# A two-layer attention and expert-lookup block: attention chunk by chunk, its second chunk inside the gather loop, and weighted sums as two products on the whole array

## The reference, cut to what matters

```python
for l in range(DEPTH):                       # 2
    proj = h @ w_in[l]                       # 1024 -> 1536: q, k, v of two branches
    oa = global_attention(rope(rms(qa)), rope(rms(ka)), va)    # 8 heads of 64, 2 kv heads
    ob = window_sink_attention(qb, kb, vb, sink[l], slopes)    # window 128, ALiBi, sink
    mix = concat(rms_norm(oa), rms_norm(ob)) @ w_o[l]
    h = layer_norm(ALPHA * h + mix)
    h = layer_norm(ALPHA * h + peer_ffn(h))

def peer_ffn(x):                             # per token
    q = x @ wq                               # 1024 -> 2048, 8 heads, two halves
    s1, s2 = top_k(q1 @ keys1, 16), top_k(q2 @ keys2, 16)
    top_s, idx = top_k(s1[:, None] + s2[None, :], 16)          # 128 experts of 16384
    a = gelu(u[idx] @ x) * softmax(top_s)
    return a @ v[idx]
```

## Time and profile before

| | us |
|---|---|
| median of 3 runs | 2925.54 (2920.96 to 2927.78) |
| the profiled execution | 2928.04 |
| its span in the profile | 2926.2 |
| first dots of layer 0 to last | 265.38 to 940.25 |
| first dots of layer 1 to last | 1160.47 to 1830.38 |

### The profile page before, as it was taken

The page is one execution under the profiler, slowest core; times in us unless marked ns, Lnnn a source line. Parts: engine busy times, 40 slices in busy tenths (PEclk is TensorE's granted clock), DMA queues, the critical chain, the costliest instruction groups (busy, mean ns, idle before and its releaser), DMA issues.

```text
span 2926.2 us, 33545 instructions
## 1 busy us (share of the span) xinstructions
PE 2148.5 (73%) x11740; PEld 1089.7 (37%) x11740; DVE 1582.8 (54%) x3254; ACT 813.4 (28%) x2292; POOL 843.2 (29%) x723
## 2 busy tenths in 40 slices
PE   6988677666766989676767666789878677667573
PEld 3657111121211559232323221568764532222221
DVE  4426857678544645888979865455552522121111
ACT  1402343433433212343343533322210111111110
POOL 1001444445432100454445553012110111222221
PEclk9889687677866989688888997899989788888887
DMA  7744999999999414999999999412112599999994
GB/s 282 263 169 159 421 422 422 420 412 395 422 422 378 194 37 160 381 421 375 413 378 403 422 421 417 159 42 74 58 62 101 210 404 401 388 391 381 382 379 146
DMA packets 130146, 891.48 MB, mean 305 GB/s; under 512 B 23216, under 2 KB 23600, under 8 KB 31792
## 3 DMA queue, kind: packets, MB, share of 16 engines
q0 software_dynamic: 86976, 553.74, 46.9%
q1 hardware_dynamic: 42992, 335.50, 28.6%
HBM read 880.21 MB, written 40.37 MB: 315 GB/s over the span
## 4 chain that ended last, share of the span: by engine, by line
PE 33%; DMA 33%; DVE 25%; ACT 4%; issue 4%; POOL 2%; SPq 1%; DVEq 0%; ACTq 0%; POOLq 0%
PE ps L155 31%; DMA ring<-in_peer_uv,idx_u 18%; DVE ring L1343 8%; DMA ring<-in_w_gu 6%; DVE arena L76 6%; DMA ring<-in_w_down 3%; ACT arena L125 3%; DMA arena<-in_w_gu 2%; PE ps L158 2%; DVE iu L113 2%; DVE arena L109 2%; DVE arena L1343 1%; DMA arena<-in_w_down 1%; DVE arena L97 1%; DMA arena<-in_peer_uv,idx_u 1%
## 5 line engine op out<-in xcount | busy, mean ns | idle before, releaser
L155 PE MATMUL ps<-ring,arena 64*64 64x512 f32 (+4 forms) x5248 | 1057.6, 764 | 475.2 <-ACT arena L125 348.0
L1343 DVE CUSTOM_DVE_ANT_0 ring<-ring,h 128x1024 f32<-128x1024 f32 x448 | 561.3, 1253 | 298.2 <-DMA ring<-in_peer_uv,idx_u 264.5
L2424 POOL DMA_INDIRECT ring<-in_peer_uv,idx_u x448 | 500.6, 1117 | 676.6 <-PE ps L155 517.4
L155 PEld LDWEIGHTS ps<-ring,arena 64*64 64x64 f32 (+3 forms) x5248 | 264.2, 158 | 1118.3 <-ACT arena L125 762.2
L155 PE MATMUL ps<-arena 128*128 128x128 f32 (+7 forms) x2760 | 471.4, 434 | 133.7 <-ACT arena L125 65.8
L125 ACT ACTIVATE arena<-arena 128x1 f32<-128x1 f32 (+3 forms) x1093 | 294.2, 269 | 812.8 <-DVE arena L1343 693.2
L155 PEld LDWEIGHTS ps<-arena 128*128 128x128 f32 (+4 forms) x2760 | 290.2, 191 | 325.4 <-ACT arena L125 150.7
L76 DVE TENSOR_TENSOR arena<-arena,ps 128x512 f32<-128x512 f32 (+1 forms) x158 | 93.6, 593 | 429.3 <-ACT arena L125 356.3
L155 PE MATMUL ps<-ring,hT 128*128 128x512 f32 (+2 forms) x896 | 310.2, 507 | 15.2 <-DVE hT L97 9.7
L125 ACT ACTIVATE arena<-ps 128x512 f32<-128x512 f32 (+5 forms) x192 | 106.4, 554 | 754.9 <-PE ps L155 707.5
L155 PEld LDWEIGHTS ps<-ring,hT 128*128 128x128 f32 x896 | 173.8, 200 | 140.9 <-issue 115.2
(11 more groups left out here) (116 smaller groups left out, 1394.6 us busy)
## 6 DMA issues: line engine op xcount, KB each, us to landing
ring<-in_w_gu SPq DMA_DIRECT2D x98, 1024.0 KB, 28.5
ring<-in_w_down SPq DMA_DIRECT2D x52, 1024.0 KB, 30.7
ring<-in_w_in SPq DMA_DIRECT2D x16, 2048.0 KB, 12.5
arena<-in_w_gu SPq DMA_DIRECT2D x30, 1024.0 KB, 29.9
ring<-in_w_mod SPq DMA_DIRECT2D x12, 2048.0 KB, 7.8
ring<-in_peer_wq SPq DMA_DIRECT2D x8, 2048.0 KB, 7.8
ring<-in_w_o SPq DMA_DIRECT2D x6, 2048.0 KB, 10.4
ring<-in_w_gates SPq DMA_DIRECT2D x12, 1024.0 KB, 4.9
```

The costliest lines, as they stand in the source:

```text
L155: return self.e.matmul(o, lhsT, rhs, start=start, stop=stop, skip_group_check=True)
L1343: v.done(v.e.tensor_tensor_reduce(out=row, in0=row, in1=h[:, n // 128, :], scale=1.0, scalar=0.0, op0=ALU.mult, op1=ALU.add, accum_out=aa[ ...
L2424: g.e.indirect_dma_start(out=landing(n), out_offset=None, in_=d["peer_uv"], in_offset=bass.IndirectOffsetOnAxis(ap=idx_u[:, n:n + 1], axis ...
```

## The change

1. `attention(l)` and the head of `peer(l)` are replaced by `first_chunk(l)`: chunk 0 alone from scores to queries and key scores, and of chunk 1 only what the other needs, the projections, keys and turned queries.
2. `second_chunk(l)`, the rest of chunk 1 (scores, powers, values, norm, output rows, layer norm, queries, key scores), becomes the first part of the background of the gather loop, one step at two n of three while n < 72.
3. `next_rows(1)`, the turned rows, projections, keys and turned queries of chunk 0 of layer 1, is the last part of the background of layer 0's loop.
4. Heads are paired in columns, so that scores of two kv heads use the two row halves of the array; the values product has the values as weights and gives the mix already turned; its mean squares come from a product with ones (`spread`).
5. The weighted sum of a gather is two products with a 128x128 diagonal, each 512 columns on the whole array.
6. Buffers move: the first block of `w_in`, the peer keys and the context's blocks go to a place in the arena (`block_p`), `w_mod` comes in halves of 1 MB into two places, and `wq` is loaded twice in each layer, once for each chunk.

```diff
 def beside(l, n):
+    if n < 72:
+        return 1 if n >= 2 and n % 3 else 0
     if l:
-        return 1 if n in range(10, 250, 3) else 0
-    return 1 if n in range(10, 246, 6) else 0
+        return 1 if n < 250 and n % 2 == 0 else 0
+    return 1 if n in range(72, LAST_ROWS, 3) or n in range(LAST_ROWS, 252, 2) else 0
...
                     for x in range(2):
-                        for r in range(2):
-                            i, o = slice(64 * r, 64 * r + 64), slice(64 * (r ^ x), 64 * (r ^ x) + 64)
-                            t = pe.mm(two[x][o, :], diagonals[n % 2][i, :], landing(n)[i, D + 512 * x:D + 512 * x + 512],
-                                      k == 0, k == 127)
+                        t = pe.mm(two[x][:, :], diagonals[n % 2], landing(l, n)[:, D + 512 * x:D + 512 * x + 512],
+                                  k == 0, k == 127)
                     pe.done(t, ("used", "gather", l, n))
...
+            def second_chunk(l):
+
+                yield
+                for br in (1, 0):
+                    scores(l, br, 1, OTHERS)
+                    yield from idle(3)
+                    turned_powers(l, br, 1, OTHERS)
+                    yield from idle(2)
+                    values(l, br, 1, OTHERS)
+                    yield
+                    spread(l, br, 1, OTHERS)
+                    yield from idle(2)
+                yield from out_rows(l, 1, OTHERS)
+                yield from idle(5)
+                turned_rows(2 * l + 1, 1, OTHERS)
+                yield
+                for hf in range(2):
+                    for i in (2 * hf, 2 * hf + 1):
+                        yield from queries(l, i, 1, OTHERS)
+                        yield
+                    key_scores(l, 1, hf, OTHERS)
+                    yield
...
             for l in range(LAYERS):
-                attention(l)
+                first_chunk(l)
                 if l:
-                    peer(l, context_states())
+                    peer(l, chain(second_chunk(l), context_states()))
                 else:
-                    peer(l, chain(context_rows(), conv_features(ctx_side, hcT, ctx_side.conv_blocks, 0, OTHERS)))
+                    peer(l, chain(second_chunk(l), context_rows(),
+                                  conv_features(ctx_side, hcT, ctx_side.conv_blocks, 0, OTHERS), next_rows(1)))
...
+                for i in range(4):
+                    block(Y_AT[l][i % 2], 4, d["peer_wq"][l, i], ("loaded", "wq", l, i, 1),
+                          after=[("used", "wq", l, i - 2, 1) if i > 1 else ("used", "w_o", l, i)])
```

More of the change, by code:

```diff
@@ L561, in attention @@
+                turned_queries(l, 1, 1, free)
+                modulation_columns(0)
+                turned_rows(2 * l + 1, 0, free)
+                for i in range(2):
+                    run(queries(l, i, 0, free))
+                key_scores(l, 0, 0, free)
                 modulation(4)
-                modulation_columns(0)
-                turned_powers(0, 0, upper)
+                run(queries(l, 2, 0, free))
                 modulation(5)
-                values(1, 0)
+                run(queries(l, 3, 0, free))
@@ new lines, in next_rows @@
+            def next_rows(l):
+                turned_rows(2 * l, 0, OTHERS)
+                yield
+                for i in range(3):
+                    yield from project(l, i, 0, OTHERS)
+                    yield
+                turned_keys(l, 1, 0, OTHERS)
+                turned_queries(l, 1, 0, OTHERS)
+                yield from idle(3)
+                turned_keys(l, 0, 0, OTHERS)
+                turned_queries(l, 0, 0, OTHERS)
+                yield
+            def peer(l, background):
@@ new lines, in next_rows @@
+            def next_rows(l):
+                take_kt(hT, ("hT", 2 * l), 0, 4)
+                a.wait_ge(*at("features stored"))
+                yield
+                yield from idle(3)
+                take_rows(l, 1, 0)
+                yield
+                yield
+                take_rows(l, 2, 0)
+                yield
+                take_keys(l, 1, 0)
+                take_queries(l, 1, 0)
+                yield from idle(3)
+                take_keys(l, 0, 0)
+                take_queries(l, 0, 0)
+                yield
@@ L2618, in rows_of, with modulate, into_p, norm_rows @@
                 return x.rearrange("(c p) n -> p c n", p=P)
-            def modulate():
-                for i in range(12):
-                    load(mod_place(i)[:, :], d["w_mod"][i], ring_sems[4 + 4 * (i % 2)], ("loaded", "w_mod", i),
-                         after=[("used", "w_mod", i - 2) if i > 1 else ("used", "w_in", 0, 1 + i)])
-            def ctx_block(i, name, before):
-                block(16, 4, d["w_in2"][i], ("loaded", "ctx", name), after=[before])
+            def modulate(*blocks):
+                for i in blocks:
+                    for half in range(2):
+                        load(mod_place(i, half)[:, :], d["w_mod"][i, :, 2048 * half:2048 * half + 2048], mod_sems[half],
+                             ("loaded", "w_mod", i, half), after=[("used", "w_mod", i - 1, half)] if i else ())
+            def into_p(src, name, after):
+                load(block_p[:, 0:src.shape[-1]], src, s_keys, name, after=after)
+            def norm_rows(r, name, l, after):
+                for x, tile in enumerate((norm_g, norm_b)):
+                    load(tile, d["rows"][r + x:r + x + 1, :].to_broadcast([P, D]), s_rows[x], ("loaded", name, l, x), after=after)
             counts = {}
@@ new lines, in sync_program @@
+                for i in range(2):
+                    block(Y_AT[l][i], 4, d["w_o"][l, i], ("loaded", "w_o", l, i), after=last)
+                into_p(d["peer_keys"][l], ("loaded", "keys", l), [("used", "w_in", l, 0)])
+                norm_rows(2 + 4 * l, "ln1", l, [("used", "ln2", 0) if l else ("used", "ln0", 0)])
+                if l == 0:
+                    modulate(1)
+                for i in range(2):
+                    block(X_AT[l][i], 4, d["peer_wq"][l, i], ("loaded", "wq", l, i, 0), after=[("used", "w_in", l, 1 + i)])
@@ new lines, in sync_program @@
+                if l:
+                    load(ctx_features, d["ctx_tab"], s_feat, ("loaded", "ctx", "features"), after=[("used", "keys", 1), ("features stored",)])
+                else:
+                    load(ctx_rows, rows_of(d["ctx"]), s_ctx, ("loaded", "ctx"), after=[("used", "wq", 0, 3, 1)])
+                    for i, (name, before) in enumerate((("Rk", ("used", "keys", 0)), ("Rv", ("used", "ctx", "Rk")),
+                                                        ("Gk", ("used", "ctx", "Rv")), ("Gv", ("used", "ctx", "Gk")))):
+                        into_p(d["w_in2"][i], ("loaded", "ctx", name), [before])
+                    into_p(d["w_in"][1, 0], ("loaded", "w_in", 1, 0), [("used", "ctx", "Gv")])
```

1080 lines of the change are left out of this document (588 added, 492 removed).

## The result

| | us |
|---|---|
| kernel before, median of the same job | 2924.74 (2920.96 to 2927.78) |
| changed kernel, median of 4 runs | 3691.43 (3687.78 to 3694.04) |
| ratio | 1.2621, 95% interval 1.2599 to 1.2643 |

The forecast was 2892, in a range of 2840 to 2952. The kernel is 26% slower, and none of the cases that the prediction priced comes near it.

What follows compares the result with a forecast made beforehand. The prediction took the gather loops as bound by DMA with 5% slack, the chain between them by PE, DVE and ACT in turn. 2928.0 - 10 - 65 + 41 = 2894 profiled, median 2892, range 2840 to 2952.

Steps and rivals of the forecast that it cites:

- the cases that the prediction priced: Forecast 2892 (chance 0.50); rivals: overlap costing almost nothing 2831 (0.15), background steps holding up gathers 2945 (0.20), lower PE clock 3063 (0.10).
- Layer 0, start: Before layer 0's gathers: first sum at 220 us, between 190 (loads hidden) and 250 (loads queue), against 276.35.
- between the layers: From layer 0's last dots to layer 1's first dots: 155.4 us in place of 220.2, a gain of 65.
- scores to mix 46, between 34 and 60: One chunk's attention before the gathers: PE work of 34 us plus waits for exponentials, scaling and the norm's power, taken as 46.
- its list there: Second chunk's work inside each gather loop: PE products and turns of 69 us, DVE some 33 us in layer 1.
- modulation blocks that wait for `in_w_mod`: Sign at layer 0's start: PE waits for modulation weights before the first sum; six half-block load waits, 29 us.
- The sum of a gather: In both gather loops: two whole-array products cost 1.81 us a gather (bounds 1.09 and 3.30), all beside transfers of 2.49.
- PE in the loops, clock 0.93: Both gather loops: PE needs some 626 us each at the upper clock; first-72-gather work was divided by a granted clock of 0.93.
- the lower clock: Rival for both loops: the granted clock stays at 0.73 to 0.85, making the kernel slower, 3063 us; chance 0.10.
- Changes of array mode: On PE in the loops: switching between 64x64 tiles and the whole array costs nothing, so dropping switches earns 0.
- Layer loops, 710 and 711: Gather loops: layer 0 takes 710 us from first sum, last dots 10 earlier; layer 1 takes 711 against 670, +41.
- lumps use up the gain: Rival for the loops: background steps stand before dots, diagonals or sums; a loop takes 737, total 2945; chance 0.20.

Runs made afterwards that it cites:

- the root kernel: The changed kernel with the POOL power in the mix norm replaced by a square root on ACT and a reciprocal on DVE, whole computation kept: 3078.47 us.
- the narrow kernels: Kernels summing each gather with four 64x64 products, such as the kernel before (2924.74 us) and the root kernel with that sum put back (3017.69 us).
- the kernel of 2987 us: The root kernel with four 64x64 products per sum, earlier load of the context's features and context steps further apart: 2987.04 us, ratio 1.0207.
- the best, at 2972.66: The kernel of 2987 us with the second chunk's 17 attention steps at every second gather and its other 30 at each gather from 38: ratio 1.0157.

## Why the prediction was wrong, by its own steps

- **Layer 0, start, and between the layers: the term that failed.** The prediction gave "scores to mix 46, between 34 and 60" with 12 us for the exponentials, "the scaling and the norm's power". The power alone is 81.9 us a branch. Eight are 656 us, 613 of the 799 us of the error, net of the cheaper root. It counted as a short wait what is an instruction on POOL that no row of PE or DVE shows; the rows that price it were POOL's. The four of the second chunk, inside the loops, it counted at nothing: its list there has PE and DVE alone. Stage by stage the changed kernel's last dots of layer 0 come at 1337 against 930, the stretch between takes 304 against 155, the loop of layer 1 950 against 711: +407, +149, +239, and +4 in the second block lead from 2894 to 3694.
- **The same two terms without the power were right.** In the root kernel the first sum comes at 229.2 against 220 (190 to 250), behind modulation blocks that wait for `in_w_mod` as forecast, and from last to first dots it is 149.1 against 155.4: the gain between the layers was 71 of a forecast 65.
- **The sum of a gather**: right, 1.88 for four records in PE's timeline above against 1.81. That it hides beside transfers was right for the kernel before (+5.8 us) and wrong here (61).
- **PE in the loops, clock 0.93**: right for the root kernel, 0.91 and 0.93, and a little high for the changed one, 0.85 and 0.87. So was the rejection of the lower clock right: 0.95 and 0.97 in the kernel before with wide sums. (That rival's terms add up to 3062, not 3063.) The Trainium skill, "TensorE: Matmul & The Clock Gate", Part 1, has the throttled state as the default, which activity releases; the granted clock of the root kernel's loop of layer 1 agrees, 0.87 in the first 72 gathers, in which PE is idle 80 of 290 us, and 0.97 behind them, where it is idle 71 of 509.
- **Changes of array mode**: in the narrow kernels tiles of 64x64 and the whole array alternate more often than in the wide ones, and they are not slower. No run isolates the drain that the Trainium skill states in "TensorEngine Tiling (Array Packing)", Key Properties. The overlap of two records in the earlier trace rows is no proof against it, since the ends of products are modelled, and this one is 0.06 us.
- **Layer loops, 710 and 711**: wrong even without the power, 801 (from the first sum) and 799. The first 72 gathers were a sum of busy time over a clock, 214 and 221 us, the others transfers with a few us for waits. The term that failed is the waiting, put at little or nothing. PE's work was sized right, 210 us in the first 72 gathers of layer 1 by the row below, but they took 290. Against the forecast the first 72 are 38 and 64 us longer and the others 53 and 24. The rival "lumps use up the gain" had the right mechanism, "each background step stands before the next dots, diagonal or sum", and priced a loop at 737; it counted only DVE's busy time and no hand-over between engines. Measured stops beyond the transfers are 221 and 185 us a layer against 47 and 31 before. By single edits from the root kernel, the time lost goes with modulation before the gathers (37, of which 30 in the loop), the wide sums (61), close context steps (29), heavy products of the second chunk (29) and the features (12), which overlap, and with the attention chain in the first 72 gathers (94, on top of root, narrow sums, spacing and load).
- **DMA share under 1 in the first 72 gathers, 1.0 in layer 0 behind them**: the first right, 0.80 and 0.84 in the root kernel, the second wrong: 0.95 there, though 1.00 in the kernel of 2987 us. First two windows of the root kernel, layer 0 behind the first 72 gathers and layer 1's first 72, then the other's:

```profile
481.00:1030.00 549.00, 453.02 (x1110) 202.60 (x1109) 332.62 (x666) 205.54 (x618) 206.46 (x195) 0.95 0.95 382
...
1179.00:1469.00 290.00, 209.64 (x720) 109.81 (x721) 170.09 (x359) 101.16 (x283) 81.04 (x76) 0.87 0.84 330
```

```profile
470.00:979.00 509.00, 346.10 (x1810) 111.07 (x1810) 333.31 (x666) 192.25 (x610) 208.51 (x192) 0.79 1.00 412
```

Taken together, the root kernel's profiled execution of 3078 us is the forecast 2894 with +100 (last dots of layer 0 at 1029.8 against 930), -6 between the layers, +88 in layer 1's loop and +2 in the second block.

In layer 0 that +100 is 9 at the first sum and 91 behind it.

What stays open: no run shows how much of the 94 us is the hand-overs and how much the 29 us of DVE's work that comes with them in each layer. And no kernel here with the whole computation and the second chunk in the loop beats the kernel before: the best, at 2972.66, gains 76 us at the start and 70 between the layers and gives 106 and 80 back in the loops (780 and 750 us against 675 and 670), with the rest of the time within 3 us.

## What to carry to other kernels

Price each new instruction by its engine, its operation and its width, also on the engine that had nothing to do; a slope from two small rows would have shown this one. Before work is moved beside a stream of transfers, count not only its busy time but how often it is handed from one engine to the next in program order: while an engine waits in such a step, its part of the stream stands too. In this kernel such waits, with those for heavy products and late loads, cost some 90 us a loop beyond the forecast, with no engine over 81% busy in a loop.

## What was not expected of the hardware

`pow` on POOL costs 0.16 us for each further column of 128 partitions: 2.90 us for 16 columns, 10.52 for 64, 20.75 for 128, 41.15 for 256, 81.9 for 512, with the exponent read from one broadcast column. A multiply of 512 columns on the same engine takes 1.48 us, 55 times less. The Trainium skill, "GPSIMD Engine Reference", 3.1, Elementwise, gives an add of two inputs as some 2.6 cycles an element and about twice DVE's time; the multiply here agrees with about that (1.48 on POOL against 0.7 on DVE), the power does not. DVE's reciprocal of 512 columns takes 3.35 us where its other operations on that size take 0.7, and PE with wide sums had a granted clock of 0.95 to 0.97 in loops in which the narrow ones had 0.73 to 0.85.
